# TensorE's loops written in line, the recurrence's norm by quarters, attention values as 64-column products

## The reference, cut to what matters

```
layer 0:  z = rmsnorm(x) @ w_in_ab
          attention: 8 heads x 64, each 64-frame chunk reads itself and the 8 chunks before it
              s = q @ k^T * scale + bias;  p = softmax(s);  att = p @ v
          convolution module: GLU -> causal depthwise conv (31) -> LayerNorm -> swish
          x += concat(att, conv) @ w_out_ab
          x += (silu(h @ Wa) * (h @ Wb)) @ Wo          hidden width 2816
layer 1:  z = rmsnorm(x) @ w_in_c  ->  q, f, v, gate;  k = 1 - f
          per head (8 heads, key 128, value 128), chunk by chunk:
              o = (decayed causal q k^T) v + (q exp(G)) S ;   S = exp(GL) S + k~ v
          o = rmsnorm(o, c_norm_g) * silu(gate);  x += o @ w_out_c
          x += swiglu(rmsnorm(x))
y = rmsnorm(x, final_norm)
```

## Time and profile before

| | us |
|---|---|
| median of 3 runs | 3137.25 (3136.32 to 3139.37) |
| the profiled execution | 3135.99, of which the span is 3134.2 |
| PE busy in the span | 2942.2 (94%) |
| DVE busy | 1435.7 (46%) |
| ACT busy | 699.5 (22%) |
| mean granted TensorE clock | 0.970 of full |

### The profile page before, as it was taken

The page is one execution under the profiler, slowest core; times in us unless marked ns, Lnnn a source line. Parts: engine busy times, 40 slices in busy tenths (PEclk is TensorE's granted clock), DMA queues, the critical chain, the costliest instruction groups (busy, mean ns, idle before and its releaser), DMA issues.

```text
span 3134.2 us, 50786 instructions
## 1 busy us (share of the span) xinstructions
PE 2942.2 (94%) x20812; PEld 2848.7 (91%) x20812; DVE 1435.7 (46%) x2474; ACT 699.5 (22%) x1148; POOL 143.8 (5%) x235
## 2 busy tenths in 40 slices
PE   5999599979999999999899999999799999999996
PEld 5998478969999999999799999989699999999996
DVE  6888675253333333334444444454623333333335
ACT  3111564131111111111322222221321111111111
POOL 4000221010000000000100000000100000000001
PEclk9999799989999999999899999999899999999998
DMA  3111321101111111111211111121111111111111
GB/s 122 41 50 64 118 104 75 47 27 48 41 41 41 48 41 41 41 47 35 88 35 50 44 53 52 42 79 44 49 43 53 36 46 41 41 41 41 41 34 61
DMA packets 51279, 163.67 MB, mean 52 GB/s; under 512 B 8480, under 2 KB 19664, under 8 KB 48512
## 3 DMA queue, kind: packets, MB, share of 16 engines
q1 hardware_dynamic: 46624, 148.98, 13.8%
q10 hardware_dynamic: 3456, 8.91, 0.8%
q0 software_dynamic: 992, 2.62, 0.4%
HBM read 143.15 MB, written 18.92 MB: 52 GB/s over the span
## 4 chain that ended last, share of the span: by engine, by line
PE 87%; DVE 7%; issue 2%; ACT 2%; DMA 1%; POOL 1%; DVEq 0%; POOLq 0%; ACTq 0%; SPq 0%
PE PS L570 20%; PE PS L571 19%; PE PS L572 19%; PE PS L812 6%; PE PS L813 6%; PE PS L814 6%; DVE HF L681 2%; PE PS L1245 1%; PE PS L1481 1%; PE PS L1596 1%; PE PS L1216 1%; PE PS L1597 1%; PE PS L1223 1%; PE PS L1598 1%; DVE HBL L691 1%
## 5 line engine op out<-in xcount | busy, mean ns | idle before, releaser
L570 PE MATMUL PS<-HAH,WH 128*128 128x384 f32 x1776 | 618.7, 348 | 15.9 <-DVE HBL L691 6.5
L571 PE MATMUL PS<-HAL,WH 128*128 128x384 f32 x1776 | 603.7, 340 | 8.5 <-issue 8.5
L572 PE MATMUL PS<-HAH,WL 128*128 128x384 f32 x1776 | 602.2, 339 | 0.0
L570 PE MATMUL PS<-HBH,WH 128*128 128x384 f32 x1776 | 595.1, 335 | 0.0
L571 PE MATMUL PS<-HBL,WH 128*128 128x384 f32 x1776 | 594.9, 335 | 0.0
L572 PE MATMUL PS<-HBH,WL 128*128 128x384 f32 x1776 | 594.8, 335 | 0.0
L558 DVE TENSOR_TENSOR WL<-WR,WH 128x1024 fp32r<-128x1024 f32 x201 | 244.1, 1223 | 586.4 <-ACT WH L553 584.8
L570 PEld LDWEIGHTS PS<-HAH,WH 128*128 128x128 f32 x1776 | 340.1, 191 | 27.7 <-issue 16.5
L812 PE MATMUL PS<-UH,WH 128*128 128x384 f32 x1056 | 357.3, 338 | 5.2 <-issue 5.0
L813 PE MATMUL PS<-UL,WH 128*128 128x384 f32 x1056 | 356.1, 337 | 0.0
L814 PE MATMUL PS<-UH,WL 128*128 128x384 f32 x1056 | 356.1, 337 | 0.0
(11 more groups left out here) (233 smaller groups left out, 2709.0 us busy)
## 6 DMA issues: line engine op xcount, KB each, us to landing
WR<-w_fi_in SPq DMA_DIRECT2D x88, 512.0 KB, 3.5
WR<-w_fo_in SPq DMA_DIRECT2D x44, 512.0 KB, 3.5
WR<-w_c_in SPq DMA_DIRECT2D x32, 512.0 KB, 4.1
WR<-w_ab_in SPq DMA_DIRECT2D x20, 512.0 KB, 3.5
CACHES<-k_cache_in SPq DMA_DIRECT2D x8, 1024.0 KB, 4.8
CACHES<-v_cache_in SPq DMA_DIRECT2D x8, 1024.0 KB, 6.9
X<-x_t_in SPq DMA_DIRECT2D x3, 1536.0 KB, 10.8
x_spill<-X SPq DMA_DIRECT2D x1, 4608.0 KB, 13.0
```

What stands on the lines that cost most here:

```text
L570: nc.tensor.matmul(out, wh, hh(k, third(n)), start=(k == 0), stop=False)
L571: nc.tensor.matmul(out, wh, hl(k, third(n)), start=False, stop=False)
L572: mm = nc.tensor.matmul(out, wl, hh(k, third(n)), start=False, stop=(k == KT - 1))
```

## The change

- All five of PE's loops become Python loops: the same instructions in the same order, written one after the other, with constants in the place of registers. ACT, DVE and SP keep theirs.
- Norm of the recurrence by quarters of 288 tokens. `norm_sums` is four products: 32 columns of ones stationary, 288 squares moving, each quarter into its own 32 partitions of bank 5 (four column positions of the array). ACT takes the root of [128, 288] into a new tile RN, DVE its reciprocal in place (`inverse`), and `norm_cast` is four products of 32 rows each (four row positions): a new constant tile `pick` with a one in the first row of each 32, moving a quarter of RN, into banks 3 to 6. `finish` has four parts of 288. The waits move with it: `norm_sums` now waits for all three `gated` parts, `norm_cast` for the streams' states (bank 6), `states` for the last `finish`. In the last head `norm_sums` stands ahead of the partial products of its step and no longer waits for their adds.
- Attention values: each 128-key tile is two products, 64 columns of V stationary and 64 probabilities moving, into partitions 0 to 63 and 64 to 127.

```diff
-            with pe.Fori(0, NCH // 2) as i:
-                T.enter(i, w0=4, w1=4, w2=4, fj=4 * N3, fb=4 * N3, u=4 * N3, x=2 * KT * N3)
+            for i in range(NCH // 2):
                 w_in(False)
                 w_out(0)
                 w_in(False)
                 w_out(1)
-                T.leave(NCH // 2)
...
                 for w in range(first_tile(s), 5):
-                    mm = nc.tensor.matmul(PS[:, out_bank(g), tile(f)], VTOK[:, c // 2 - 4 + w, tile(f)], PRT[:, s % 2, tile(w)],
-                                          start=(w == first_tile(s)), stop=(w == 4))
+                    for e in range(2):
+                        v0, p0 = f * P + CHK * e, w * P + CHK * e
+                        mm = nc.tensor.matmul(PS[CHK * e:CHK * (e + 1), out_bank(g), v0:v0 + CHK],
+                                              VTOK[:, c // 2 - 4 + w, v0:v0 + CHK], PRT[:, s % 2, p0:p0 + CHK],
+                                              start=(w == first_tile(s)), stop=(w == 4))
...
             def norm_sums():
                 need(pe, s_oq, T("hgrn") * N3 + N3)
-                need(pe, s_vk, T("vk"))
-                for t in range(NT):
-                    mm = nc.tensor.matmul(PS[:, 2, TH + t:TH + t + 1], AM[:, t, :], ones[:, 0:1], start=True, stop=True)
+                need(pe, s_og, T("hgrn") * N3 + N3)
+                squares = AM[:, :, :].rearrange("p a b -> p (a b)")
+                for g in range(QN):
+                    mm = nc.tensor.matmul(PS[BLK * g:BLK * (g + 1), 5, 0:QTOK], ones[:, 0:BLK], squares[:, quarter(g)], start=True, stop=True)
                 mm.then_inc(s_cm, 1)
 
             def norm_cast():
                 need(pe, s_cd, T("hgrn") + 1)
-                need(pe, s_og, T("hgrn") * N3 + N3)
-                for n in range(N3):
-                    mm = nc.tensor.matmul(PS[:, 3 + n, 0:TH], ones[:, :],
-                                          KD[:, TPT * n:TPT * n + TPT, :].rearrange("p a b -> p (a b)"), start=True, stop=True)
-                    mm.then_inc(s_cb, 1)
+                need(pe, s_sn, (T("hgrn") + 1) * NB)
+                for g in range(QN):
+                    r = slice(BLK * g, BLK * (g + 1))
+                    mm = nc.tensor.matmul(PS[:, 3 + g, 0:QTOK], pick[r, :], RN[r, :], start=True, stop=True)
+                mm.then_inc(s_cb, 1)
...
-                act.activation(rt[:, 0:NT], PS[:, 2, TH:TH + NT], ACT.Sqrt, bias=eps[:, 0:1], scale=1.0 / P).then_inc(s_cr, 1)
+                act.activation(RN[:, :], PS[:, 5, 0:QTOK], ACT.Sqrt, bias=eps[:, 0:1], scale=1.0 / P).then_inc(s_cr, 1)
...
-            def diagonal():
+            def inverse():
                 need(dve, s_cr, T("hgrn") + 1)
-                link(dve, T, dve.reciprocal(ri[:, 0:NT], rt[:, 0:NT]))
-                dve.tensor_tensor(KD[:, :, :], ident[:, :].unsqueeze(1).to_broadcast([P, NT, P]),
-                                  ri[:, 0:NT].unsqueeze(2).to_broadcast([P, NT, P]), ALU.mult).then_inc(s_cd, 1)
+                dve.reciprocal(RN[:, :], RN[:, :]).then_inc(s_cd, 1)
 
             def finish(h):
-                for n in range(N3):
-                    need(dve, s_cb, T("hgrn") * N3 + n + 1)
-                    o = X[:, h, third(n)]
-                    dve.scalar_tensor_tensor(out=o, in0=o, scalar=sm("gn"), in1=PS[:, 3 + n, 0:TH], op0=ALU.mult,
+                need(dve, s_cb, T("hgrn") + 1)
+                for g in range(QN):
+                    o = X[:, h, quarter(g)]
+                    dve.scalar_tensor_tensor(out=o, in0=o, scalar=sm("gn"), in1=PS[:, 3 + g, 0:QTOK], op0=ALU.mult,
                                              op1=ALU.mult).then_inc(s_cn, 1)
```

More of the change, by code:

```diff
@@ L63 @@
 NARROW = 5
+QN = P // BLK
+QTOK = TOK // QN
 SMALL = dict(cw=(0, AB * CW), cb=(124, AB), lg=(128, AB), lb=(132, AB), gain=(136, 5 * KT),
@@ L134, in encoder @@
         eps = sb("eps", [P, 1])
+        pick = sb("pick", [P, P])
         with ExitStack() as c2:
@@ L178, in encoder @@
             ADG = s2("ADG", [P, NT, BLK])
+            RN = s2("RN", [P, QTOK])
             TA = s2("TA", [P, TOK // 2])
@@ L734, in proj_pe @@
             block(1, True)
-            with pe.Fori(0, KT // 2 - 1) as i:
-                T.enter(i, w0=1, w1=1, x=2 * N3)
+            for i in range(KT // 2 - 1):
                 block(0, False)
                 block(1, False)
-                T.leave(KT // 2 - 1)
         def proj_act(act, T):
@@ L974, in ab_pe @@
             step(normed(pe, T, 0))
-            with pe.Fori(0, AB - 1) as i:
-                T.enter(i, w0=2, w1=2, w2=1, g=N3, a=N3, q=N3, k=N3, v=N3, vt=N3)
+            for i in range(AB - 1):
                 step()
-                T.leave(AB - 1)
         def ab_act(act, T):
@@ L1441, in level_bank, with quarter @@
             return 3 + lv % 2
+        def quarter(g):
+            return slice(g * QTOK, (g + 1) * QTOK)
         def state_bank(b):
@@ L1461, in vturn @@
                 T.add("vk")
-                if n == 0:
-                    need(pe, s_cr, T("hgrn"))
                 for tt in range(TPT):
@@ L1471, in level @@
                 if lv == 0:
-                    need(pe, s_cn, T("hgrn") * N3)
+                    need(pe, s_cn, T("hgrn") * QN)
                 need(pe, s_mg, T("mg") - 1)
@@ L1585, in c_pe @@
             step(1, 0)
-            with pe.Fori(0, CH // 2 - 1) as i:
-                T.enter(i, w0=2, w1=4, w2=2, up=2 * (LEVELS + 2), mg=2 * (LEVELS + 1), kt=2 * N3, vk=2 * N3, head=2, hgrn=2, sf=2)
+            for i in range(CH // 2 - 1):
                 step(0, 1)
                 step(1, 0)
-                T.leave(CH // 2 - 1)
             def opening(out, slot, n, stop):
@@ L1640, in c_pe @@
                     sample_states()
+                if i == 10:
+                    norm_sums()
                 for j in (2 * i, 2 * i + 1):
@@ L1715, in root @@
                 need(act, s_cm, T("hgrn") + 1)
-                act.activation(rt[:, 0:NT], PS[:, 2, TH:TH + NT], ACT.Sqrt, bias=eps[:, 0:1], scale=1.0 / P).then_inc(s_cr, 1)
+                need(act, s_cd, T("hgrn"))
+                act.activation(RN[:, :], PS[:, 5, 0:QTOK], ACT.Sqrt, bias=eps[:, 0:1], scale=1.0 / P).then_inc(s_cr, 1)
             def diagonal_blocks():
@@ L1772, in c_act @@
             act.wait_ge(s_cf["g"], N3 * CH)
-            act.wait_ge(s_cn, N3 * (CH - 1))
+            act.wait_ge(s_cn, QN * (CH - 1))
             for n in range(N3):
@@ L1797, in c_act @@
             for n in range(N3):
-                need(act, s_cn, N3 * (CH - 1) + n + 1)
+                need(act, s_cn, QN * (CH - 1) + n + 2)
                 act.activation(HBH[:, AB - 1, third(n)], X[:, PART, third(n)], ACT.Copy).then_inc(s_hhi, 1)
@@ L1937, in step @@
                         if i == 11:
-                            diagonal()
+                            inverse()
                     if pp is not None and k == "g":
@@ L1946, in c_dve @@
             with dve.Fori(0, CH // 2 - 1) as i:
-                T.enter(i, hi=8, gs=2 * N3, dc=2 * (1 + LEVELS + 1 + 1), lv=2 * (LEVELS + 1), mg=2 * (LEVELS + 1),
+                T.enter(i, hi=8, gs=2 * N3, dc=2 * (1 + LEVELS + 1), lv=2 * (LEVELS + 1), mg=2 * (LEVELS + 1),
                         ss=2 * PT_TILES, hgrn=2)
@@ L2080, in _ @@
             dve.memset(eps[:, :], EPS).then_inc(s_low, 1)
+            link(dve, T, dve.memset(pick[:, :], 0.0))
+            for g in range(QN):
+                ins = dve.memset(pick[BLK * g:BLK * g + 1, :], 1.0)
+            link(dve, T, ins)
             dve.wait_ge(s_small, 16)
```

3 lines of the change are left out of this document (removed).

## The result

| | us |
|---|---|
| before, median of 4 runs | 3137.3 (3136.3 to 3139.4) |
| changed kernel, median of 4 runs | 3094.1 (3092.4 to 3097.0) |
| ratio | 0.9862, 95% interval 0.9845 to 0.9879 |
| profiled execution, before and after | 3135.99 and 3096.99 (span 3095.3) |

The kernel is 43 us faster. 3103 was forecast, with a range of 3090 to 3120: right in sign and range, 9 us short. The profiled execution is the slowest of the four, 2.9 above their median, so the traces show 39 of the 43.

The account below looks back on a forecast made before the run. PE was taken to bound the kernel, DVE and ACT under half busy in feed-forward and recurrence. Savings 20.5 + 10.5 + 0.5 + 2 = 33.5 us from 3135.99 gave 3102.5, forecast as 3103; range 3090 to 3120.

Parts of the forecast that it names:

- Pauses of the loops: Feed-forwards, both layers: straight code removes 12 pauses at jumps back, 13.8 us, with follow-on costs 19.5 us.
- Refill and clock behind the long pauses: Feed-forwards: array filling again after 12 pauses, 1.2 us, and three half-clock stretches behind jumps, 4.5 us.
- The pause that stays: Last feed-forward pass: PE's wait for ACT's and DVE's weight cut remains, about 2.5 us per layer.
- Other loops: First projection, output projection and recurrence, two jumps each: 0.2 us per jump, 1 us in all.
- Straight code at nothing: PE's written-out program: bringing the longer code to the engine costs no time.
- the slower rival: PE's whole program: straight code brought too late, pauses of 0.6 to 0.7 us per packet, 3220 us; chance 0.04.
- Sums: Recurrence norm: four products in four positions take 0.62 us instead of 1.93, saving 1.31 per head, 10.5 over eight.
- Cast: Recurrence norm: 1.3 us saved becomes 0.1 per head in six heads, as PE waits some 0.9 for DVE's KC.
- The inverse: Recurrence norm, DVE's reciprocal of 288 columns: 2.4 us, adding a wait of 0.1 to 0.3 inside PE's existing 0.9.
- Heads: Recurrence, all norm terms together: 1.31 x 8 + 0.5 = 11 us faster.
- its spread: Forecast's allowance for recurrence half-clock stretches, five inside heads: none or eight would move the time by -8 or +5 us.
- Values: Attention values in two positions: five-tile items gain 0.17 us each, short ones lose; +2 us in all, bounds +12 and -10.

Follow-up runs that it names:

- the repeated one: The changed kernel run once more without an edit, beside the follow-up kernels: median 3094.8 us, against 3133.2 for the kernel before.
- sample states later: Changed kernel with DVE's KC behind the inverse, 128-column short attention items, and sample-state products one product later: 3088.7 us, ratio 0.9853.
- KC first: Changed kernel with DVE making the next head's KC behind the inverse, not `finish`, and short attention items at 128 columns: 3096.2 us, ratio 0.9875.

## Why the prediction was right, and where its sizes were off

- **Pauses of the loops, 13.8 + 1.2 + 4.5 = 19.5.** Right: the loop alone gave 21.4 by the medians, 3.4 in layer 0 and 18.2 in layer 1. Refill and clock behind the long pauses were needed for it: the bare pauses are 13.8.
- **The pause that stays** is there in both layers, 2.5 each.
- **Other loops, 1.** 0.6 to 1.4, inside the spread. The recurrence's two jumps alone were 1.0 in the kernel before.
- **Straight code at nothing.** Right: no pause of the short kind appeared; the slower rival is out. There was even less to bring, 168 packets where the loops took 179, but that is the feed-forward's part: with its loop alone in line the queue moved 161, with all five 165. The three other loops brought less as loops than in line. With them kept, 161 packets are fewer than the 162.6 that 20,812 matmuls and as many loads would fill, so some code ran again without being brought again.
- **Sums, 1.31 each.** 0.62 as forecast to the hundredth, and 0.45 for four more. **Cast, 0.1 each, with 0.9 of waiting.** 0.86, and a second cast is free. The mechanism is right, the match of the wait partly luck: the prediction's own terms, 1.3 less the lead of 0.28 and with KC 0.12 later, make 1.1, and the cast brought PE only 1.06 nearer to the level (from cast to level, waits left out, 5.14 where it was 6.20), since the product between them kept its slow start. The inverse was put at 2.4 and took 1.95: (1952 - 156) / 287 = 6.3 ns per element where one to nine elements gave 7.8. It hid all the same.
- **Heads, 11.** In the whole change they gave 17.2. Of the difference of 6, three half-clock stretches fewer are 4.7, which the prediction left in its spread (-8 to +5): of the five inside the heads only two were left. The recurrence's jumps, which the prediction has among the other loops, are 1.0. The 11.2 of the norm alone are no proof of the 11, as said above.
- **Values, +2.** The item is as forecast (0.73 and 2.45), and from first score to last values the stage gained 1.8 in the profiled run, 3.6 in the repeated one and 2.2 alone. But from first score to layer 0's first `w_out` it was 422.7 both before and after and 420.8 in the repeat: what attention gained came back between it and the feed-forward. So 0 to 2, and the term's size stays open.
- **The 8.9 us beyond the forecast.** In the profiled runs 5.5: heads +6.2, feed-forwards +2.1 (21.6 against 19.5), other loops and values -3. The other 3.4 are distances from the median: 2.9 of the profiled run of the changed kernel, the rest rounding and the 1.3 of before.

One thing the prediction did not see, although its rows had it: the 8.5 us at L571 were the price of where this loop's head lay, not of a jump as such. The step "four pauses of 8.5" came out, but the norm or the values alone removed them too. That is why the parts do not add. 22.8 + 21.8 + 12.7 = 57.3 for a change worth 43; each holds the same 14.9 of layer 1, and with that counted once 27.5 are left. Of the 15.7 between that and 43, the profiles put 7.5 in the heads (17.2 together, 0.6 + 11.2 - 2.1 = 9.7 apart). That is not the clock, which in the heads gave the parts more than the whole: by half-clock stretches one, three and two fewer apart, three fewer together. Most of it is the recurrence's jumps: the norm alone and the values alone lost 5.6 and 5.0 us at them, where the kernel before lost 1.0 and the changed one nothing. Whole against parts that makes +8.7; half-clock stretches make -4.7, the waits for KC that the pauses of the norm alone hide -1.7, what lies behind the seventh head's sums +4.0, and some 1 stays open. That these pauses are the bringing of code, as in layer 1, was not tested. Another 5 lie in the time to the first score, which, counted from PE's first matmul, varies from 325.8 to 329.2 among kernels whose start is the same. The last 3 stay open, within the spread of the runs. Nor was it tried what sets the clock in the heads apart from the place of the sample states.

## What to carry to other kernels

A pause called "issue" just behind a jump back, and a second one a few instructions on, are the bringing of code: their size depends on the loop head's place in its packet, so an unrelated edit moves them. Such a pause can stand under another engine's name, as in the norm alone: look whether PE started the same piece elsewhere without that wait. Before crediting a gain of 0.5% to an edit, compare the stages that it does not touch. A saving in a stage bound by TensorE counts only if the granted clock holds: break up runs of thin matmuls with dense ones, and read the clock of the stretch before and after.

## What the runs showed of the hardware

- A jump back in the feed-forward cost 0.4 to 0.9 us of pause; in layer 1 of the kernel before, 1.8 to 2.3 more, four matmuls on. Padding by 32 matmuls with their loads removed the second pause, by 128 or 256 brought it back. At the recurrence's jumps it was 0.4 to 0.6 before, 2.6 to 3.0 with the norm alone, and 2.8 and 1.8 six matmuls on with the values alone.
- With only the feed-forward's loop in line the instruction queue moved 161 packets, fewer than the 162.6 that the matmuls and loads would fill; with all loops 179, with none 165.
- Four products of 288 columns in four column positions took 0.62 with the changes of shape, and four more 0.45; in four row positions 0.69. Ten 64-column products in two positions took 0.73, where five of 128 columns took 1.11.
- Half clock behind thin matmuls repeats from head to head or stays away as a whole: six heads of 70.61 (sample states later) or five of 71.58 (changed kernel) without any, or five in a row of 72.3 and 73.9 with one and two in each (KC first).
- The kernel before moved by 13 us between runs (3130 to 3144) with no edit at all.
